# Second attention of a two-layer step in head pairs: value tiles stationary over both latent tiles, output written turned, norm weights as scales of copies

## The chip, the cores and the metric

The kernel runs on one core of one Trainium2 chip. The metric is the device time of one execution in microseconds, the median of several runs. A profiled execution gives the span, the busy time of each engine and the rows quoted below.

## The reference

Two token streams go through two layers: 128 prompt tokens and 256 sample tokens, 1024 features, all in fp32. Layer 0 mixes with a gated long convolution and grouped attention. Layer 1 mixes with latent attention (MLA), and each layer ends with 16 experts, two per token. What matters here is the mixer of layer 1:

```python
c_q, c_kv, k_rope = split(h @ od_w_in)                # 256, 128, 32
c_q, c_kv = rmsnorm(c_q, gq), rmsnorm(c_kv, gkv)
q = rmsnorm((c_q @ w_uq).reshape(n, 16, 96), q_norm)
k_nope, v = split((c_kv @ w_ukv).reshape(n, 16, 128)) # 64 and 64 per head
k = rmsnorm(concat(k_nope, broadcast(k_rope)), k_norm)
q, k = rope_tail(q, 64), rope_tail(k, 64)             # sample tokens only, last 32
o = softmax(q @ k.T * 96 ** -0.5) @ v                 # prompt: 128 keys; sample: 128 cached + 256
y = o.reshape(n, 1024) @ od_w_out
```

Prompt tokens see the 128 prompt keys. Sample tokens see 128 cached keys (made from a cached latent and a cached rotary part, without rotation) and their own 256.

## The kernel before

Five engines run instruction lists written by hand, joined by semaphores. Tokens stand in three tiles of 128: tile 0 is the prompt, tiles 1 and 2 are the sample (here "latent tiles"). PSUM has eight banks; `Banks.stage` (lines 174 to 184) lists which bank each job takes, `claim` (818) makes TensorE wait until its last user has drained it, and `filled_wait`, `drained_wait` and `drain_inc` are the other ends. Matmuls all pass through `product` (line 841), transposes ("turns") through `turn` (848) and ScalarE's plain copies through `copy_out` (1500), so these lines gather many jobs in the profile; the tile names tell them apart. An fp32 product leaves two records in the trace, a turn one.

Weights come in pieces of 1 MB through a ring of nine slots on SyncE's queue, each sent when the piece nine before it has been used (lines 654 to 658); `send_early` (660) puts five pieces of expert weights into the arena, in layer 1 once the attention's last results (`mO3`) are drained.

The stage of interest starts behind the norm of the latents (DVE lines 2402 to 2412). TensorE turns the latents (`cT`), then works on four groups of four heads (`HG`). `project(g)` (1406) makes queries (3 tiles of 384 columns, two contraction steps) and keys (4 tiles of 256 columns) of group g; ScalarE copies them into `q4s[g % 2]` and `k4s[g % 2]`. VectorE's `mla_norm` (1918) has 12 steps: square and sum of queries and of keys (steps 0 to 3, with the rotary part of the keys copied in first), reciprocal of the root (4), and then `mla_turn` (624): on the keys a product with the reciprocal, one with the weights of the norm, and the rotation of two tiles (8 to 11); GpSimd does the same on the queries (4 to 7). `MLA_NORM_AT` (85) says behind which unit of the present group's attention each step for the next group stands in VectorE's queue.

In group g TensorE makes the values (`project_kv(g, "mv", ...)`), waits for `qk_ready` and `qk_turned`, turns 12 query and 16 key tiles of 128x96, waits for ScalarE's copies of these, projects group g+1 and then runs `attention` (958) over 12 units (tile, head). A unit is: scores (queries stationary, 128 or 384 keys moving), maximum on VectorE (1873), exp with a sum on ScalarE (1551), turn of the probabilities on TensorE, copy to SBUF on VectorE (1868), and the product with the values: the turned probabilities are stationary and 64 value columns move, one product per key tile. Behind the fourth head of a tile VectorE divides by the sums (1884) and writes tokens by features into `mtok`. Each stage has two buffers. One step of the modulation products (`mod_step("mla", ...)`, 1024x512 weights) stands behind unit 3 of each group; it also has a selecting part of 16 narrow records.

After the last group 24 turns and six copies bring `mtok` into `hT`, features by tokens (1457 to 1464), and `moe(1)` begins with the output product (`out_tile`, 921), prompt tile first.

Layer 0's attention (`pair_scores`, `pair_turn`, `tile_values`, `sums_turn`, `sums_spread`, lines 996 to 1031, and `tile_mask`, `tile_join` on VectorE) already goes by pairs of heads: the values are stationary, 64 wide, in two halves of the array, and the probabilities of four heads (512 columns) move. The result comes out turned, so the division needs the sums along the columns: reciprocals are turned, masked into eight rows and spread over 128 partitions by a product with `half_rows`.

## Time and profile before

| | |
|---|---|
| median of 3 runs | 1047.16 us |
| range of the runs | 1043.32 to 1048.2 us |
| the profiled execution | 1041.73 us |
| its span | 1039.9 us |
| mean granted clock of TensorE | 0.898 of 2.4 GHz |
| busy: TensorE, VectorE, ScalarE, GpSimd | 875.4, 397.9, 270.3, 92.7 us |
| second attention, first key or query turned to first output product | 614.8 to 789.7 us |

The busy times are sums over stages with different limits, and idle time of an engine costs only where another waits for it. A timeline row gives the start and length of a run of like instructions; the bracket behind it is the idle time before it and what ended that.

### The profile page before, as it was taken

The page shows a single profiled execution, that of the slowest core. Times are in us where ns is not written, and L with a number is a line of the kernel's source. Part 1 is how long each engine was busy: PE and PEld are TensorE (multiplying, and loading weights), DVE is VectorE, ACT ScalarE, POOL GpSimd, SP SyncE. Part 2 cuts the span into 40 slices and gives each one's busy share as a digit, 9 for nine tenths or more (in the row PEclk, how much of TensorE's full clock was granted, in tenths as well). Part 3 has the DMA queues.
Part 4 walks back from the last instruction along what each step waited for, and adds up shares of the span by engine and source line. Part 5 has one row for each costly group of instructions (what it writes and reads, how often), then busy time and mean ns, then how long its engine had stood idle before and what let it go on. Part 6 is the DMA issues. An engine that isn't in the chain of part 4 may idle for free.

```text
span 1039.9 us, 12183 instructions
## 1 busy us (share of the span) xinstructions
PE 875.4 (84%) x4419; PEld 509.4 (49%) x4419; DVE 397.9 (38%) x854; ACT 270.3 (26%) x624; POOL 92.7 (9%) x120
## 2 busy tenths in 40 slices
PE   2898999998989979997767778878789999998760
PEld 0345765535534555553324446656675565554320
DVE  1468182353342424221115157383732342321114
ACT  1134012200531332221124244333341232221111
POOL 1000000000000030000030032130300012000002
PEclk9997999999889979999966898887879987999995
DMA  8980244344900499999999462020106188999975
GB/s 237 382 283 1 81 128 162 110 162 108 380 38 1 158 336 380 413 411 410 367 393 390 150 243 81 1 82 1 41 1 243 65 316 299 397 411 411 388 267 192
DMA packets 86417, 231.79 MB, mean 223 GB/s; under 512 B 8832, under 2 KB 18561, under 8 KB 86041
## 3 DMA queue, kind: packets, MB, share of 16 engines
q1 hardware_dynamic: 72418, 193.88, 50.5%
q0 software_dynamic: 7616, 26.95, 7.3%
q10 hardware_dynamic: 6328, 10.23, 2.7%
q8 instruction: 35, 0.57, 0.2%
q14 instruction: 20, 0.16, 0.0%
HBM read 216.40 MB, written 17.52 MB: 225 GB/s over the span
## 4 chain that ended last, share of the span: by engine, by line
PE 60%; DMA 16%; DVE 8%; issue 5%; ACT 5%; DVEq 3%; SPq 2%; ACTq 1%; POOLq 0%; POOL 0%
PE ps L841 54%; DMA ring<-in_moe_w_up_dram 7%; DMA ring<-in_w_mod_dram 5%; PE ps L848 4%; DVEq L1805 3%; DMA arena<-in_moe_w_up_dram 2%; SPq L658 1%; PE ps L1044 1%; ACT arena L1500 1%; ACTq L641 1%; DMA arena<-in_moe_w_down_dram 1%; ACT hT L1531 1%; DMA hT<-h_rows,rows_in 1%; DVE negmax L1873 1%; DVE statA L1938 1%
## 5 line engine op out<-in xcount | busy, mean ns | idle before, releaser
L841 PE MATMUL ps<-arena 128*64 128x256 f32 (+12 forms) x1332 | 290.6, 445 | 39.1 <-DVE arena L1868 10.6
L841 PEld LDWEIGHTS ps<-arena 128*64 128x64 f32 (+4 forms) x1332 | 170.6, 188 | 141.9 <-issue 68.5
L841 PE MATMUL ps<-ring,hT 128*128 128x512 f32 (+2 forms) x384 | 136.8, 517 | 7.8 <-ACT hT L1531 3.6
L841 PE MATMUL ps<-ring,arena 128*64 128x256 f32 (+1 forms) x864 | 125.0, 432 | 16.3 <-DMA ring<-in_moe_w_up_dram 8.3
L841 PEld LDWEIGHTS ps<-ring,hT 128*128 128x128 f32 x384 | 74.7, 196 | 66.4 <-issue 61.5
L841 PEld LDWEIGHTS ps<-ring,arena 128*64 128x64 f32 x864 | 60.8, 136 | 66.1 <-issue 39.6
L841 PE MATMUL ps<-ring,condT 128*32 128x512 f32 x384 | 63.9, 784 | 25.2 <-DMA ring<-in_w_mod_dram 19.1
L1500 ACT ACTIVATE arena<-ps 128x256 f32<-128x256 f32 (+6 forms) x94 | 43.9, 497 | 133.4 <-PE ps L841 120.5
L848 PE MATMUL ps<-ident,arena 128*128 128x128 f32 (+2 forms) x276 | 51.7, 319 | 24.9 <-ACT arena L1551 11.0
L2139 DVE TENSOR_TENSOR arena<-arena,ps 128x128 f32<-128x128 f32 x37 | 10.6, 288 | 138.1 <-ACT arena L1578 138.1
L841 PE MATMUL ps<-hT,ring 128*128 128x384 f32 x192 | 62.1, 486 | 0.0
L848 PEld LDWEIGHTS ps<-ident,arena 128*128 128x128 f32 (+2 forms) x276 | 37.2, 163 | 36.3 <-issue 22.9
L2142 DVE COPY arena<-ps 64x512 f32<-64x512 f32 x37 | 25.7, 693 | 65.7 <-PE ps L841 65.7
L841 PEld LDWEIGHTS ps<-hT,ring 128*128 128x128 f32 x192 | 36.5, 190 | 25.2
L1584 ACT ACTIVATE arena<-ps 64x512 f32<-64x512 f32 x37 | 21.8, 589 | 78.2 <-PE ps L841 78.2
L1873 DVE TENSOR_REDUCE negmax<-ps 128x1 f32<-128x384 f32 (+1 forms) x48 | 22.0, 462 | 51.2 <-PE ps L841 50.4
L841 PEld LDWEIGHTS ps<-ring,condT 128*32 128x32 f32 x384 | 11.0, 128 | 61.3 <-issue 30.7
L1551 ACT ACTIVATE arena<-ps,negmax 128x384 f32<-128x384 f32 (+1 forms) x48 | 24.3, 508 | 63.6 <-DVE negmax L1873 63.4
L1578 ACT ACTIVATE arena<-ps 128x128 f32<-128x128 f32 x37 | 10.3, 277 | 90.7 <-PE ps L841 90.7
L1958 DVE TENSOR_TENSOR arena<-ps,gb 128x512 f32<-128x512 f32 x12 | 8.3, 691 | 63.4 <-PE ps L841 63.4
L1531 ACT ACTIVATE hT<-ps,modT,modA 128x128 f32<-128x128 f32 x48 | 17.7, 464 | 45.4 <-PE ps L848 42.5
L641 POOL DMA_DIRECT2D arena<-in_before_dram x2 | 1.1, 563 | 313.0 <-DVE hT L1967 313.0
(284 smaller groups left out, 918.5 us busy)
## 6 DMA issues: line engine op xcount, KB each, us to landing
ring<-in_w_mod_dram SPq DMA_DIRECT2D x48, 1024.0 KB, 10.4
ring<-in_moe_w_down_dram SPq DMA_DIRECT2D x24, 1024.0 KB, 18.1
ring<-in_moe_w_gate_dram SPq DMA_DIRECT2D x42, 512.0 KB, 14.0
ring<-in_moe_w_up_dram SPq DMA_DIRECT2D x42, 512.0 KB, 16.5
arena<-in_moe_w_gate_dram SPq DMA_DIRECT2D x32, 512.0 KB, 8.0
arena<-in_moe_w_up_dram SPq DMA_DIRECT2D x32, 512.0 KB, 9.9
arena<-in_moe_w_down_dram SPq DMA_DIRECT2D x13, 1024.0 KB, 13.4
ring<-in_ev_w_in_dram SPq DMA_DIRECT2D x9, 1024.0 KB, 12.3
```

The lines of the kernel that those rows point to most:

```text
L641: eng.dma_start(dst, src).then_inc(s, 16)
L658: sp.dma_start(ring_view(i, shape, off)[rows], src).then_inc(piece_full[i % RING], 16)
L841: mm = pe.matmul(out, lhsT, rhs, **kw)
L848: mm = pe.transpose(out, src, ident[:, :])
L1500: drain_inc(act.activation(dst, src, kw.pop("func", ACT.Copy), **kw), stage, i)
L1531: ins = act.activation(hT[:, k, t * P:(t + 1) * P], bank[:, k * P:(k + 1) * P], ACT.Identity, bias=modT[:, l, SH2 if which else SH1, k, GR ...
L1551: ins = act.activation(pr[:, i % 2, 0:nk], bank[:, 0:nk], ACT.Exp, bias=negmax[:, i:i + 1], accum_out=psumexp[:, i:i + 1])
L1584: act.activation(dst, ps[Y_BANKS[e % 2]][0:HALF, :], ACT.Copy).then_inc(done[l], 1)
L1805: dve.drain()
L1873: dve.tensor_reduce(negmax[:, i:i + 1], bank[:, 0:nk], AXX, ALU.max, negate=True).then_inc(negmax_ready, 1)
L2139: dve.tensor_tensor(mid[:, e % 2, :], sil[:, e % 2, :], ps[GU_BANKS[e % 2]][:, P:2 * P], ALU.mult).then_inc(mid_ready[l], 1)
L2142: dve.tensor_copy(dst, ps[Y_BANKS[e % 2]][HALF:P, :]).then_inc(y_read[1][l], 1)
```

## The change

It touches layer 1's mixer only.

- Attention goes by six pairs of heads per group, `MLA_PAIRS` = (tile, pair): both prompt pairs first, then tiles 1 and 2 of pair 0, then of pair 1. Each engine has its own `mla_attention` with the order of rounds written out. Scores have four banks in place of two.
- The turned probabilities are kept for both latent tiles (`turned_m`), and one product per key tile and head has the values as the stationary operand, 64 wide in one half of the array, and 256 columns moving (`mla_values`). The prompt's are 128 wide (`mla_values_prompt`).
- The result comes out as features by tokens and is written straight into `hT` (`mla_join`); `mtok`, its 24 turns and six copies are gone, and `out_tile` waits for `mO` itself. The division by the sums goes as in layer 0: reciprocal, turn, mask, spread, copy, join, once for the prompt and once for the latent tiles of a group.
- Of the copies of turned probabilities, the second of every odd pair is ScalarE's.
- The norm weights of the first 64 features, and 96 ** -0.5, are no longer multiplied in by VectorE and GpSimd: they are a scale by partition (`head_gain`) of the copies of turned queries and keys. The rotary weights are folded into tables made once (`mla_tables`): `kp`, the keys' rotary part with weight and rotation, `kp2`, its sum of squares, and `qtab`, the queries' rotation table. `mla_norm` has 7 steps, which cover 64 of the 96 features of a key. The loads of norm weights grow by two: `mgain` is loaded as two rows of 32, `head_gain` as two columns.
- Keys are turned before queries, `project(g+1)` comes before the wait for the copies, the last two key copies are VectorE's, there is one buffer each for queries and keys, and the modulation step stands at the end of a group's attention, between the turn of the sums and the last value products.

The core of the diff (views of buffers, banks, loads and removed bodies are left out):

```diff
-MLA_NORM_STEPS = 12
-MLA_NORM_AT = {1: (0,), 2: (1,), 3: (2,), 4: (3,), 7: (4,), 8: (8,), 9: (9,), 10: (10,), 11: (11,)}
+MLA_NORM_STEPS = 7
+MLA_NORM_AT = {0: 0, 1: 1, 2: 2, 3: 3, 5: 4, 6: 5, 7: 6}
 MLA_AHEAD = 3
+MLA_PAIRS = [(0, 0), (0, 1), (1, 0), (2, 0), (1, 1), (2, 1)]
+MLA_KEYS = (3, 1, 2)
...
+def mla_column(i, r):
+    t, p = MLA_PAIRS[i]
+    return 4 * r + 2 * p + (QH + t - 1 if t else 0)
+def mla_turned(g, i, r, src):
+    t, p = MLA_PAIRS[i]
+    if t == 0:
+        return hT[:, 2 * g + p, P + P * r:2 * P + P * r], src
+    return turned_m[:, p, :, r, P * (t - 1):P * t], src.rearrange("p (a b) -> p a b", b=P)
...
-            for step in range(4, 8):
-                mla_turn(pool, g, step, (msq[:, 0, :, 0:ROPE], msq[:, 1, :, 0:ROPE]))
-                if step == 7:
-                    pool.drain().then_inc(qk_turned, 1)
-                else:
-                    pool.drain()
+            flat = q4.rearrange("p t h e -> p (t h) e")
+            pool.tensor_tensor(flat, flat, statA[:, 1, 0:NT * HG].unsqueeze(2).broadcast_to([P, NT * HG, QK]), ALU.mult)
+            for t in range(1, NT):
+                pool.drain()
+                rope(pool, q4[:, t, :, NOPE:QK], qtab[:, t - 1, :, :], mrb[:, 0, :, :], mrb[:, 1, :, :], HG, ROPE)
+            pool.drain().then_inc(qk_turned, 1)
...
+        else:
+            for g in range(NHG):
+                drained_wait(pe, f"mO{g}", min(t, 1))
...
+    def mla_scores(g, i):
+        t, p = MLA_PAIRS[i]
+        for r in range(2):
+            bank = claim(f"mS{g}", 2 * i + r)
+            keys = k4T[:, 2 * p + r, 0, :] if t == 0 else k4T[:, 2 * p + r, 1:4, :].rearrange("p a b -> p (a b)")
+            fill_inc(product(bank[:, 0:P if t == 0 else T], q4T[:, t, 2 * p + r, :], keys, start=True, stop=True), f"mS{g}", 2 * i + r)
+    def mla_turns(g, i):
+        for r in range(2):
+            bank = claim(f"mPT{g}", 2 * i + r)
+            drained_wait(pe, f"mS{g}", 2 * i + r)
+            for s in range(1 if MLA_PAIRS[i][0] == 0 else NT):
+                mm = turn(bank[:, s * P:(s + 1) * P], mprobs[:, i % 2, r, s * P:(s + 1) * P])
+            fill_inc(mm, f"mPT{g}", 2 * i + r)
+    def mla_values_prompt(g):
+        for u in range(4):
+            drained_wait(pe, f"mPT{g}", u)
+        bank = claim(f"mO{g}", 0)
+        for p in range(2):
+            for r in range(2):
+                mm = product(bank[HD * r:HD * r + HD, P * p:P * p + P], v4[:, 0, 2 * p + r, :], hT[:, 2 * g + p, P + P * r:2 * P + P * r], start=True, stop=True)
+        fill_inc(mm, f"mO{g}", 0)
+    def mla_values(g, p):
+        for u in range(4 * p + 4, 4 * p + 8):
+            drained_wait(pe, f"mPT{g}", u)
+        bank = claim(f"mO{g}", 1) if p == 0 else ps[B[f"mO{g}", 1][0]]
+        for s, t in enumerate(MLA_KEYS):
+            for r in range(2):
+                mm = product(bank[HD * r:HD * r + HD, NSA * p:NSA * p + NSA], v4[:, t, 2 * p + r, :], turned_m[:, p, s, r, :], start=s == 0, stop=s == NT - 1)
+        if p == 1:
+            fill_inc(mm, f"mO{g}", 1)
+    def mla_sums_turn(g, part):
+        pe.wait_ge(sums_ready, NT + 2 * g + part + 1)
+        fill_inc(turn(claim(f"mL{g}", 2 * part)[0:QH, 0:P], rinv[:, 0:QH]), f"mL{g}", 2 * part)
+    def mla_sums_spread(g, part):
+        n = 512 if part else NSA
+        fill_inc(product(claim(f"mL{g}", 2 * part + 1)[:, 0:n], half_rows, masked_m[:, 0:n], start=True, stop=True), f"mL{g}", 2 * part + 1)
+    def mla_attention(g):
+        n = len(MLA_PAIRS)
+        for i in range(n + 2):
+            if i >= 2:
+                mla_turns(g, i - 2)
+            if i == 5:
+                mla_sums_spread(g, 0)
+                mla_scores(g, i)
+            if i == 4:
+                mla_sums_turn(g, 0)
+                mla_values_prompt(g)
+            if i == 6:
+                mla_values(g, 0)
+        mla_sums_turn(g, 1)
+        mod_step("mla", MLA_AHEAD + g)
+        mla_values(g, 1)
+        mla_sums_spread(g, 1)
...
-        q4, k4 = q4s[g % 2], k4s[g % 2]
         project_kv(g, "mv", NOPE)
         pe.wait_ge(qk_ready, NT + 1 + g)
+        for s, t in enumerate((0,) + MLA_KEYS):
+            bank = claim(f"mkT{g}", s)
+            for h in range(HG):
+                mm = turn(bank[0:QK, h * P:(h + 1) * P], k4[:, t, h, :])
+            fill_inc(mm, f"mkT{g}", s)
         pe.wait_ge(qk_turned, g + 1)
         for t in range(NT):
             bank = claim(f"mqT{g}", t)
             for h in range(HG):
                 mm = turn(bank[0:QK, h * P:(h + 1) * P], q4[:, t, h, :])
             fill_inc(mm, f"mqT{g}", t)
-        for s, t in enumerate((0, 3, 1, 2)):
-            bank = claim(f"mkT{g}", s)
-                mm = turn(bank[0:QK, h * P:(h + 1) * P], k4[:, t, h, :])
-            fill_inc(mm, f"mkT{g}", s)
+        if g + 1 < NHG:
+            project(g + 1)
         for t in range(NT):
             drained_wait(pe, f"mqT{g}", t)
         for t in range(NT + 1):
             drained_wait(pe, f"mkT{g}", t)
-        if g + 1 < NHG:
-            project(g + 1)
         for t in range(NT + 1):
             drained_wait(pe, f"mv{g}", t)
-        attention(str(g), units_mla, HG, lambda t, h: q4T[:, t, h, :],
-                  lambda t, h: k4T[:, h, 0, :] if t == 0 else k4T[:, h, 1:4, :].rearrange("p a b -> p (a b)"),
-                  lambda t, h: [v4[:, s, h, :] for s in ((0,) if t == 0 else (3, 1, 2))])
-    for g in range(NHG):
-        for t in range(NT):
-            drained_wait(pe, f"mO{g}", t)
-    for t in range(NT):
-        for q in range(2):
-            bank = claim("moT", 2 * t + q)
-                mm = turn(bank[:, c * P:(c + 1) * P], mtok[:, t, (4 * q + c) * P:(4 * q + c + 1) * P])
-            fill_inc(mm, "moT", 2 * t + q)
-    for i in range(2 * NT):
-        drained_wait(pe, "moT", i)
+        mla_attention(g)
...
+    def mla_probs(g, i):
+        nk = P if MLA_PAIRS[i][0] == 0 else T
+        for r in range(2):
+            u, c = 2 * i + r, mla_column(i, r)
+            act.wait_ge(negmax_ready, 2 * NPAIRS + 2 * len(MLA_PAIRS) * g + u + 1)
+                filled_wait(act, f"mPT{g}", u - 4)
+            drain_inc(act.activation(mprobs[:, i % 2, r, 0:nk], bank_of(f"mS{g}", u)[:, 0:nk], ACT.Exp, bias=negmax[:, c:c + 1], accum_out=psumexp[:, c:c + 1]), f"mS{g}", u)
+    def mla_copy(g, i):
+        nk = P if MLA_PAIRS[i][0] == 0 else T
+        copy_out(f"mPT{g}", 2 * i + 1, *mla_turned(g, i, 1, bank_of(f"mPT{g}", 2 * i + 1)[:, 0:nk]))
+    def mla_reci(g, part):
+        n = 512 if part else NSA
+        if g or part:
+            drained_wait(act, f"mO{g if part else g - 1}", 1 - part)
+        copy_out(f"mL{g}", 2 * part + 1, reci_m[:, 0:n], bank_of(f"mL{g}", 2 * part + 1)[:, 0:n])
+    def mla_attention(g):
+        n = len(MLA_PAIRS)
+        for i in range(n + 2):
+            if i >= 2 and i % 2:
+                mla_copy(g, i - 2)
+            if i == 5:
+                mla_reci(g, 0)
+            if i < n:
+                mla_probs(g, i)
+            if g + 1 < NHG and i == 4:
+                mla_root(g + 1)
+        mod_step("mla", MLA_AHEAD + g)
+        mla_reci(g, 1)
...
+        for s in range(2):
+            copy_out(f"mkT{g}", s, k4T[:, :, s, :], bank_of(f"mkT{g}", s)[0:QK, :].rearrange("p (a b) -> p a b", b=P), scale=head_gain[:, 2:3])
         for t in range(NT):
-            copy_out(f"mqT{g}", t, q4T[:, t, :, :].rearrange("p a b -> p (a b)"), bank_of(f"mqT{g}", t)[0:QK, :])
-        for s in range(NT + 1):
...
+    def mla_max(g, i):
+        nk = P if MLA_PAIRS[i][0] == 0 else T
+        for r in range(2):
+            c = mla_column(i, r)
+            bank = filled_wait(dve, f"mS{g}", 2 * i + r)
+            dve.tensor_reduce(negmax[:, c:c + 1], bank[:, 0:nk], AXX, ALU.max, negate=True).then_inc(negmax_ready, 1)
+    def mla_copy(g, i):
+        nk = P if MLA_PAIRS[i][0] == 0 else T
+        for r in range(2 - i % 2):
+            bank = filled_wait(dve, f"mPT{g}", 2 * i + r)
+            drain_inc(dve.tensor_copy(*mla_turned(g, i, r, bank[:, 0:nk])), f"mPT{g}", 2 * i + r)
+    def mla_sums(g, part):
+        last = 2 * len(MLA_PAIRS) if part else 4
+        for u in (last - 2, last - 1):
+            drained_wait(dve, f"mS{g}", u)
+        dve.reciprocal(rinv[:, 0:QH], psumexp[:, QH * part:QH * part + QH]).then_inc(sums_ready, 1)
+    def mla_mask(g, part):
+        bank = filled_wait(dve, f"mL{g}", 2 * part)
+        columns = own_column if part else own_column[:, 0::2]
+        n = 4 if part else 2
+        shape = [QH, n, P]
+        drain_inc(dve.tensor_tensor(masked_m[:, 0:n * P].rearrange("p (a b) -> p a b", b=P), bank[0:QH, 0:P].unsqueeze(1).broadcast_to(shape),
+                                    columns.unsqueeze(2).broadcast_to(shape), ALU.mult), f"mL{g}", 2 * part)
+    def mla_join(g, part):
+        bank = filled_wait(dve, f"mO{g}", part)
+        drained_wait(dve, f"mL{g}", 2 * part + 1)
+        n = NSA if part else P
+        by_head = lambda a: a[:, 0:2 * n].rearrange("p (a b) -> p a b", b=n)
+        cols = slice(P, T) if part else slice(0, P)
+        drain_inc(dve.tensor_tensor(hT[:, 2 * g:2 * g + 2, cols], by_head(bank), by_head(reci_m), ALU.mult), f"mO{g}", part)
+    def mla_attention(g):
+        n = len(MLA_PAIRS)
+        for i in range(n + 2):
+            if i == 6:
+                mla_join(g, 0)
+            if i >= 2:
+                mla_copy(g, i - 2)
+            if i == 3:
+                mla_sums(g, 0)
+                mla_max(g, i)
+            if i == 4:
+                mla_mask(g, 0)
+            if i == 7:
+                mla_sums(g, 1)
+            if g + 1 < NHG and i in MLA_NORM_AT:
+                mla_norm(g + 1, MLA_NORM_AT[i])
+        mla_mask(g, 1)
+        mod_step("mla", MLA_AHEAD + g)
+        mla_join(g, 1)
...
-        q4, k4 = q4s[g % 2], k4s[g % 2]
         flat = lambda a: a.rearrange("p t h e -> p (t h) e")
+        k_nope = flat(k4)[:, :, 0:NOPE]
+        by_nope = msq[:, 0:nkk * NOPE].rearrange("p (a e) -> p a e", e=NOPE)
+        by_key = lambda which: statA[:, which, nq:nq + nkk].rearrange("p (t h) -> p t h", h=HG)
         settle()
         if step == 0:
             for t in range(NT):
                 drained_wait(dve, f"mq{g}", t)
-            for t in range(NT + 1):
-                kr = kr_c if t == NT else um[:, t, QR + KVR:ODD_IN]
-                dve.tensor_copy(k4[:, t, :, NOPE:QK], kr.unsqueeze(1).broadcast_to([P, HG, ROPE]))
-            dve.tensor_tensor(flat(msq)[:, 0:nq, :], flat(q4), flat(q4), ALU.mult)
+            dve.tensor_tensor(msq.rearrange("p (a e) -> p a e", e=QK), flat(q4), flat(q4), ALU.mult)
         elif step == 1:
-            dve.tensor_reduce(statA[:, 0, 0:nq], flat(msq)[:, 0:nq, :], AXX, ALU.add)
+            dve.tensor_reduce(statA[:, 0, 0:nq], msq.rearrange("p (a e) -> p a e", e=QK), AXX, ALU.add)
         elif step == 2:
             for t in range(NT + 1):
                 drained_wait(dve, f"mk{g}", t)
-            dve.tensor_tensor(flat(msq), flat(k4), flat(k4), ALU.mult)
+            dve.tensor_tensor(by_nope, k_nope, k_nope, ALU.mult)
         elif step == 3:
-            dve.tensor_reduce(statA[:, 0, nq:nq + nkk], flat(msq), AXX, ALU.add)
+            dve.tensor_reduce(statA[:, 0, nq:nq + nkk], by_nope, AXX, ALU.add)
+            settle()
+            dve.tensor_tensor(by_key(0), by_key(0), kp2.unsqueeze(2).broadcast_to([P, NT + 1, HG]), ALU.add)
             settle()
             dve.tensor_scalar(statA[:, 0, 0:28], statA[:, 0, 0:28], 1.0 / QK, EPS, ALU.mult, ALU.add).then_inc(qvar, 1)
         elif step == 4:
             dve.wait_ge(qroot, 2 + g)
             dve.reciprocal(statA[:, 1, 0:28], statA[:, 1, 0:28]).then_inc(inv_root, 1)
+        elif step == 5:
+            dve.tensor_tensor(k_nope, k_nope, statA[:, 1, nq:nq + nkk].unsqueeze(2).broadcast_to([P, nkk, NOPE]), ALU.mult)
+        else:
+            shape = [P, NT + 1, HG, ROPE]
+            dve.tensor_tensor(k4[:, :, :, NOPE:QK], kp.unsqueeze(2).broadcast_to(shape), by_key(1).unsqueeze(3).broadcast_to(shape), ALU.mult)
+            dve.drain().then_inc(qk_ready, 1)
...
+    mla_tables()
     for step in range(MLA_NORM_STEPS):
         mla_norm(0, step)
+    for i in range(MLA_AHEAD):
+        mod_step("mla", i)
     for g in range(NHG):
-        attention(str(g), units_mla, HG,
-                  lambda t, g=g: mtok[:, t, g * HG * VD:(g + 1) * HG * VD].rearrange("p (h e) -> p h e", e=VD))
+        for s in range(2, NT + 1):
+            bank = filled_wait(dve, f"mkT{g}", s)
+            drain_inc(dve.tensor_scalar(k4T[:, :, s, :], bank[0:QK, :].rearrange("p (a b) -> p a b", b=P), head_gain[:, 2:3], None, ALU.mult), f"mkT{g}", s)
+        mla_attention(g)
```

## Rows read from the trace of the kernel before

**Rows 1.** The page's 40 slices of 26 us: busy share of the DMA engines, in tenths.
```profile
DMA  8980244344900499999999462020106188999975
```

**Rows 2.** Stretches of the second attention, busy us of each engine, clock, DMA share, GB/s.
```profile
core 0: us, PE busy (x) PEld busy (x) DVE busy (x) ACT busy (x) POOL busy (x), PEclk, DMA share, GB/s
583.60:614.80 31.20, 23.31 (x108) 12.18 (x108) 20.14 (x26) 10.30 (x23) 10.22 (x12) 0.89 0.74 267
614.80:663.40 48.60, 40.71 (x199) 30.41 (x200) 26.46 (x51) 19.68 (x46) 10.39 (x10) 0.79 0.13 47
663.40:711.40 48.00, 39.72 (x200) 29.02 (x199) 26.70 (x51) 18.38 (x46) 10.39 (x10) 0.82 0.13 44
711.40:759.20 47.80, 39.09 (x199) 28.36 (x198) 26.46 (x51) 18.36 (x46) 10.39 (x10) 0.82 0.07 23
759.20:789.70 30.50, 26.17 (x177) 22.32 (x176) 12.79 (x33) 14.03 (x38) 0.00 (x0) 0.89 0.09 26
```

**Rows 3.** TensorE's waits in the second group, 663.4 to 711.4: total us, times, longest.
```profile
PE ps L841 <- DVE arena L1868: 3.8, 3, 1.7
PE ps L848 <- ACT arena L1551: 3.1, 5, 1.1
PE ps L841 <- ACT arena L1500: 1.2, 1, 1.2
```

**Rows 4.** The chain that ended last: a steady head of the last group; layer 1's output products.
```profile
777.26 0.34 PE ps L848 x3
777.60 1.26 PE ps L841 x8
...
789.72 27.70 PE ps L841 x64
```

**Rows 5.** Timeline of layer 0's value products, TensorE: start, us, instruction.
```profile
295.07 1.08 PE L841 MATMUL ps<-arena,cv 128*64 128x512 f32 x4
295.98 1.89 PE L841 MATMUL ps<-arena 128*64 128x512 f32 x8
```

**Rows 6.** Timeline, TensorE: a modulation step's two parts.
```profile
604.62 1.92 PE L841 MATMUL ps<-ring,condT 128*32 128x512 f32 x16
...
633.48 2.08 PE L841 MATMUL ps<-rowsel,modrow 128*64 128x2 f32 x16
```

**Rows 7.** Groups of the second group's stretch, shapes apart: busy us, mean ns, idle before.
```profile
L1868 DVE COPY arena<-ps 128x384 f32<-128x384 f32 x8 | 4.4, 550 | 0.4 <-PE ps L841 0.2 <-issue 0.2
...
L633 POOL TENSOR_TENSOR arena<-arena 128x1152 f32<-128x1152 f32 x1 | 4.0, 3953 | 0.1
...
L633 DVE TENSOR_TENSOR arena<-arena 128x1536 f32<-128x1536 f32 x1 | 3.1, 3076 | 0.1
...
L631 DVE TENSOR_TENSOR arena<-arena,statA 128x1536 f32<-128x1536 f32 x1 | 2.5, 2531 | 0.1
...
L631 POOL TENSOR_TENSOR arena<-arena,statA 128x1152 f32<-128x1152 f32 x1 | 2.1, 2112 | 36.9 <-DVE statA L1943 36.9
...
L1936 DVE TENSOR_TENSOR arena<-arena 128x1536 f32<-128x1536 f32 x1 | 1.8, 1757 | 0.3 <-issue 0.3
...
L1539 ACT ACT_TABLE_LOAD x1 | 1.3, 1283 | 0.0
```

**Rows 8.** Timeline of the lead-in: a load on GpSimd, VectorE's first norm step, TensorE's first turns.
```profile
538.07 0.58 POOL L641 DMA_DIRECT2D arena<-in_rope_m_dram  x1
...
595.18 0.81 DVE L1929 COPY arena<-arena 128x128 f32<-128x128 f32 x4 [9.51 <-ACT arena L1500]
...
609.27 1.99 PE L841 MATMUL ps<-arena 128*128 128x256 f32 x8 [0.69 <-ACT gb L1500]
614.82 4.93 PE L848 MATMUL ps<-ident,arena 128*96 128x128 f32 x28 [3.55 <-DVEq L1948]
```

**Rows 9.** Timeline of the stage's end: last division, turns, first output product.
```profile
784.98 0.42 DVE L1884 TENSOR_TENSOR xn<-ps,rinv 128x256 f32<-128x256 f32 x1 [0.89 <-PE ps L841]
...
785.66 2.81 PE L848 MATMUL ps<-ident,xn 128*128 128x128 f32 x24 [0.71 <-DVE xn L1884]
...
789.72 1.53 PE L841 MATMUL ps<-ring,hT 128*128 128x512 f32 x3 [1.25 <-ACT hT L1500]
```

**Rows 10.** The stretch of layer 0's attention, columns as in rows 2.
```profile
270.00:311.00 41.00, 34.32 (x143) 15.26 (x142) 21.51 (x53) 16.14 (x56) 0.00 (x0) 0.79 0.46 181
```

197 lines of the change are left out of this document (56 added, 141 removed).

## The prediction

> **What bounds the kernel now.** I began with the page's table of 40 slices [rows 1]: the DMA engines stand at 9 from about 365 us and at 8 or 9 again from about 830 us, in the two expert stages; between 575 and 780 us the digits are 0 to 6, mostly 0 to 2. The second attention is not a transfer stage. The stretches [rows 2] cut it at the first turned query of each group of four heads: 31.2 us of lead-in, three groups of 48.6, 48.0 and 47.8, and 30.5 to the first output product, 206.1 us together. In a group TensorE is busy 40 of 48 us, VectorE 26.5, ScalarE 18 to 20, GpSimd 10.4. So TensorE bounds the group, but not at its full pace: the granted clock is 0.79 to 0.82, and since it has two levels, 2.4 and 1.2 GHz, a mean of 0.82 is 36% of the time at the lower. That is 17 us of each 48, and 62 us from 614.8 on (20.4+17.3+17.2+6.7). The waits of one group [rows 3] name VectorE's copies of the turned probabilities (3.8 us), the exps (3.1) and the copies of the keys (1.2). VectorE is late because the next group's norm work (squares, sums, scale, gain, rotation) stands in its queue between a maximum and a copy. In the last group, which has no norm work, a head of a latent tile takes a steady 1.60 us [rows 4].
>
> **TensorE's work, at full clock.** 64 records of 512 columns take 27.70 us [rows 4], 0.433 each; a product of fp32 is two records, so 384 columns cost 0.64, 256 cost 0.43, 128 cost 0.21. In 1.60 us a head does three turns (0.35), a score product (0.64) and three value products [rows 4], which leaves 0.61 for those: 0.20 each for 64 moving columns.
> Removed: per group 8x0.61 + 4x0.20 = 5.7 us of value products. Added: the values are stationary, 64 wide, with 256 moving columns. Layer 0 has this form: 8 records of 64x512 took 1.89 us and 4 took 1.08 [rows 5], about 0.22 a record, half of 0.433, so the two halves of the array work at once. 256 columns are then 0.11 a record, 24 records of the latent tiles 2.6 us, the prompt's 0.5. Nearly half is saved there, but the sums of the exps must now be turned and spread (two turns at 0.25, a spread of 512 columns at 0.87 and one of 256 at 0.43: 1.8 us together). Scores (8x0.64+4x0.21=6.0), turns of probabilities (3.3), of queries and keys (3.3), the value projection (1.7), the next projections (5.5) and the modulation (1.92 and 2.08 [rows 6] and 0.2) stay. Per group: 6.0+3.3+3.3+1.7+5.5+4.2+3.1+1.8 = 28.9 us, against 29.7 before. The work hardly shrinks; the gain must come from waits and clock.
>
> A rule of the Trainium skill speaks against the change (TensorEngine Tiling (Array Packing), Key Properties): a change of tiling mode drains TensorE. Layer 0's rows after such a change [rows 5] show 1.08 us for four records where 0.87 is the steady price, so 0.2 at most. With six changes a group the rule at that price would put 4.8 us on the sum.
>
> **VectorE and GpSimd.** VectorE loses the gain of the keys (3.08 us), a third of their squares and sums (1.2 of twice 1.76), three of twelve copies of probabilities (1.4 at 0.55 and less) [rows 7], both rotations and the copies of the rotary part (about 3); it gains two copies of turned keys (0.7 each, the 0.55 of 384 columns scaled to 512), the mask and wider joins (0.8 more). From 26.5 [rows 2] it comes to about 20. GpSimd loses the gain (3.95). ScalarE takes the three copies and two of reciprocals: plus 2.5 on 18 to 20, hidden beside TensorE. The scale factor within copies costs nothing: the copy is there already, and it streams the same elements; were a scaled copy dearer by a tenth, 0.3 us a group, it would lie beside the projections. The tables built once (some 24 small VectorE operations, 3.5 us at 0.15 each) fall into a wait of VectorE of 9.51 us [rows 8]. The two further small loads of weights are issued on GpSimd's queue near 538 us, at 0.58 each [rows 8], and wanted at 583: 44 us of cover; beyond it, each microsecond late is one lost.
>
> **The first start.** Before, TensorE was free at 609.27+1.99 = 611.26 and waited until 614.82 for the rotations [rows 8]. Root and reciprocal come about 1.5 us earlier, at 602; of GpSimd's 10.4 us a group [rows 2] 3.95 go, so it is done by 610 with its pauses, and the keys, turned first now, by 606. The start moves to 611.3: 3.5 saved.
>
> **One group in queue order.** I set out the new instructions of each engine in their order, with the durations above, 0.2 us for a hand-over to TensorE, 0.12 to VectorE, 0.15 to ScalarE (before: maximum to exp 0.04 to 0.2, exp to turn 0.1 to 0.3). TensorE then waits: 0.9 for the first exps; 1.5 for the second pair's, whose maxima stand behind the square of the queries (1.35 us, three quarters of the 1.76 [rows 7]); 1.1 and 0.9 for the third's and fourth's, behind a sum and the squares of the keys; 1.1 for the mask, before the prompt's spread; 1.9 for a copy that ScalarE does after its change of tables for the root (2x1.28 us [rows 7]); 2.6 for the last reciprocal, behind the scale of the keys on VectorE. Together 10.0, and 28.9+10.0 = 38.9 us a group. Before, by the same procedure, 43.6. The wait for the key copies ahead of the projections (1.2 [rows 3]) is gone, since the projections now come first. The tail of the last group (sums, mask, spread, copy, join) is followed by the prompt's output product, which doesn't need it.
> The old stage's end: last join, 24 turns and six copies, 784.98 to 789.72 [rows 9], 4.7 us, falls away whole. The last group has no norm, root or projection: 3.2 for turns, 1.0 for their copies, 16.4 for attention and half a modulation, 1.8 of waits: 22.4.
> At full clock: 27.7 + 3x38.9 + 22.4 = 166.8 us. The old one by this procedure was 31.2 (measured) + 160.1; measured were 174.9 for the latter, so 14.8 us are the price of 62 us at the low clock, 0.24 per us. In the new stage the ladder's beginning and the narrow modulation products will still bring the clock down; the stretch of some 10 us at a low clock after each group's late copies and 64-column values should go in part. I take 40 us, 9.6 us of price. The stage: 166.8+9.6 = 176.4, against 206.1: 29.7 saved.
> The bounds: waits of 6 to 14 us a group (12 each way), 15 to 75 us at the low clock (3.6 to 18 us). Extremes are 47 and 9 saved; 8 in 10 I set at 15 to 43.
>
> **What follows the stage.** The expert stage starts its transfers when output weights are freed and when the last join is done, so it moves as a block. The early weights (asked for right after the last join before, ahead of the output products) start some 5 us later against them; they are wanted over 60 us later.
>
> **The total.** The profiled execution took 1041.73 us, its span 1039.9, 5.4 below the median of 1047.16. It would come to 1012; from the median, 1047.2-29.7 gives 1017.5, which I forecast, with 1004 to 1032. A measurement of this kernel tells about 0.5%, 5 us, from no change.
>
> **Rivals.** (a) The pair form carries its own stalls. Layer 0's attention took 41.0 us for 24 head tiles at a clock of 0.79 [rows 10], 20.5 for twelve. Without its packed rows the scores cost 3 more, the modulation 4.2, norm and root about 4, the rest of the group 10.5: 42.2, and with the mask and norms colliding 45. Then 3.5 + 3x3.1 + 5.5 = 18 saved: 1029. For it: the same order of work on VectorE. Against: the join and ScalarE's copy of the reciprocals come earlier in the round here. Chance 0.25. (b) The clock stays up and the waits stay at 6: 42 saved, 1005; chance 0.12. (c) The expert stage, at a DMA share of 9 in [rows 1], gives most of it back, as its transfers can't come earlier: 1040; against it, every such transfer waits for an event of this stage. Chance 0.04. (d) Slower: the clock. With TensorE's gaps short but frequent, it could stay at 1.2 GHz through all four rounds. From 166.8, the gain of 39 is used up when 164 us at the low clock cost 0.24 each; where TensorE has no wait left to cover it the price is 0.5, and 80 us suffice. All four attention parts at the low clock double some 18 us of work each, 74 us, less some 24 of waits that this swallows: 50, and 1047-39+50 = 1058. The rows speak against so much: projections ran at full clock in every group. Chance 0.02. (e) That it doesn't do what it says: the turned result would need another pass; the join writes straight into the tile that the output product reads, so this gets no chance. The forecast has the remaining 0.57; the range leaves out c, d and about half of b.
> The Trainium skill (SBUF — State Buffer, Who interferes with whom) has VectorE and GpSimd lock each other out of a shared port. The keys' scale of 2.53 us beside GpSimd's 2.11 agrees, against 1.76 for a product as large alone [rows 7]; by full exclusion the new scale would wait 2.1 us, 1.3 more than I took, 5 us in all.
>
> **What would show it.** Right: turns of keys at 611 us with no wait for GpSimd; groups of 40 to 44 us; value products of 64x256 at 0.11 a record at full clock; the first output product 2 us or less after the last spread; VectorE near 20 us a group; the expert stage unchanged in length. Wrong: groups over 45; waits over 3 us for the mask, the join or ScalarE's table change; a mean clock at 0.75 or less; a longer expert stage.
> Chances: faster by over 0.5%, 0.94 (forecast, a, b, and most of c); within 0.5%, 0.04; slower 0.02.

## The result, and the profile after

In four runs each the changed kernel took **1000.19 us** (995.23 to 1004.56), the kernel before 1045.24 (1040.76 to 1048.2): ratio 0.957, 95% interval 0.951 to 0.963. The forecast was 1017.5, its range 1004 to 1032: the change gave more than the range held. Ratios leave out two slow runs of the experiments: one of the kernel before (1055.34 us, beside x1 to x4) and one of x14 (1002.6 us). The profiled execution of the changed kernel took 1004.56 us, its span 1002.7. The page's granted clock and DMA lines, 40 slices of 25 us:

```profile
PEclk9997999999888997999885679998998998999995
DMA  7990236235850088999989946112106289999975
```

The groups lie in the 25th to 30th slice, where DMA stands at 0 to 2 but for the first; the clock is at 9 there, once at 8, and its low digits 5, 6, 7 stand ahead of them. The stretches, columns as in [rows 2]: to the first turned latent, the lead-in, the four groups, the rest.

```profile
0.00:592.05 592.05, 508.80 (x2385) 277.68 (x2386) 219.55 (x479) 138.81 (x316) 32.60 (x54) 0.91 0.66 237
592.05:617.13 25.08, 24.20 (x108) 13.16 (x109) 12.43 (x32) 9.88 (x22) 5.18 (x9) 0.81 0.69 245
617.13:654.96 37.83, 32.56 (x181) 21.20 (x180) 20.47 (x39) 20.66 (x51) 6.10 (x9) 0.95 0.33 117
654.96:693.70 38.74, 34.04 (x182) 21.84 (x181) 20.48 (x39) 19.49 (x50) 6.11 (x9) 0.91 0.16 55
693.70:730.32 36.62, 32.44 (x182) 21.22 (x181) 20.52 (x39) 19.38 (x50) 6.11 (x9) 0.95 0.09 31
730.32:755.49 25.17, 22.78 (x135) 15.11 (x133) 12.56 (x31) 11.83 (x35) 0.00 (x0) 0.92 0.01 1
755.49:1002.70 247.21, 196.68 (x1157) 106.06 (x1156) 68.13 (x171) 51.23 (x110) 20.96 (x28) 0.91 0.83 314
```

From here "the stage" runs from the first turned latent to the first output product: 163.4 us here, 203.9 before (585.78 to 789.72). The 40.5 us divide into the lead-in 4.0 (29.0 before by this cut), three groups 31.2 (144.4 to 113.2) and the last group 5.3 (30.5 to 25.2).

What changed inside the three groups? With the low clock counted as in the prediction, they had 54.9 us of it before (20.4+17.3+17.2) and have 14.5 now. Busy time less half the low time is TensorE's work at full rate: 92.0 us before, 91.9 now. So the work is the same within what this reckoning can tell (three profiles of the changed kernel give 91.9, 91.1 and 92.6); 20.2 us of the difference are booked under the clock and 10.7 under pauses (24.9 to 14.2). This is bookkeeping: a pause that the low clock hides comes back at full clock, so taking the low clock away gives less than half of its time, as the prices below show. What the form of the value products saves in work (2.8 us a group by x3 below) is spent again, on turning and spreading the sums among others; the gain is made elsewhere.

The second group of the changed kernel, TensorE's timeline (start, length, instruction, idle time before it):

```profile
664.97 0.65 PE L845 MATMUL ps<-ident,arena 128*128 128x128 f32 x2 [0.29 <-ACT arena L1557]
665.46 1.46 PE L838 MATMUL ps<-arena 96*128 96x384 f32 x4
668.21 0.53 PE L845 MATMUL ps<-ident,arena 128*128 128x128 f32 x2 [1.29 <-DVE hT L1882]
...
671.02 0.87 PE L845 MATMUL ps<-ident,arena 128*128 128x128 f32 x6 [0.99 <-DVE hT L1882]
...
677.44 2.93 PE L838 MATMUL ps<-arena 96*128 96x384 f32 x4
680.16 1.49 PE L845 MATMUL ps<-ident,arena 128*128 128x128 f32 x6
681.80 2.24 PE L838 MATMUL ps<-xn,arena 128*64 128x256 f32 x12 [0.16 <-DVE hT L1904]
```

Four score records take 1.46 us at full clock and 2.93 at the low one; here the low stretch is some 7 us, behind pauses of 1.29, 0.99, 0.77 and 0.70 us. The same four pauses stand in the second group of x13, another profile of the same kernel, and there the clock stays at 1.00: the pauses alone don't settle it.

### The profile page after: what moved, and what is told of

Same layout as the page of the kernel before. It is cut to its first block, busy times and chain, and to the rows that moved or that the text cites. A ratio compares the mean times of both kernels' runs of the same rounds, so it can differ in the third digit from the quotient of the medians.

```text
span 1002.7 us, 11944 instructions
## 1 busy us (share of the span) xinstructions
PE 851.5 (85%) x4323; PEld 476.3 (47%) x4323; DVE 374.1 (37%) x829; ACT 271.3 (27%) x630; POOL 77.1 (8%) x118
## 4 chain that ended last, share of the span: by engine, by line
PE 63%; DMA 18%; DVE 7%; issue 4%; ACT 3%; SPq 2%; ACTq 2%; DVEq 1%; POOLq 0%; POOL 0%
PE ps L838 56%; DMA ring<-in_w_mod_dram 5%; DMA ring<-in_moe_w_up_dram 5%; PE ps L845 4%; DMA ring<-in_moe_w_down_dram 2%; DMA h_rows<-xn 2%; DMA arena<-in_moe_w_up_dram 2%; PE ps L1067 2%; ACTq L636 1%; SPq L653 1%; DVE negmax L1876 1%; DVEq L1826 1%; ACT hT L1540 1%; DMA hT<-h_rows,rows_in 1%; DVE xn L1882 1%
## 5 line engine op out<-in xcount | busy, mean ns | idle before, releaser
L838 PE MATMUL ps<-arena 128*64 128x256 f32 (+13 forms) x1108 | 244.6, 462 | 20.5 <-DVE arena L2082 5.2
L838 PEld LDWEIGHTS ps<-arena 128*64 128x64 f32 (+4 forms) x1108 | 127.5, 172 | 114.9 <-issue 71.7
L838 PE MATMUL ps<-ring,arena 128*64 128x256 f32 (+1 forms) x864 | 129.7, 444 | 16.4 <-DMA ring<-in_moe_w_down_dram 8.4
L838 PE MATMUL ps<-ring,condT 128*32 128x512 f32 x384 | 59.9, 737 | 26.9 <-DMA ring<-in_w_mod_dram 20.5
L1509 ACT ACTIVATE arena<-ps 128x256 f32<-128x256 f32 (+5 forms) x88 | 39.2, 452 | 132.6 <-PE ps L838 123.8
L845 PEld LDWEIGHTS ps<-ident,arena 128*128 128x128 f32 (+2 forms) x332 | 41.4, 148 | 38.8 <-issue 18.5
L2207 DVE TENSOR_TENSOR arena<-arena,ps 128x128 f32<-128x128 f32 x37 | 10.7, 288 | 131.6 <-ACT arena L1602 131.6
L838 PEld LDWEIGHTS ps<-hT,ring 128*128 128x128 f32 x192 | 36.6, 190 | 25.1
L838 PEld LDWEIGHTS ps<-ring,condT 128*32 128x32 f32 x384 | 10.4, 121 | 61.7 <-issue 28.4
L838 PE MATMUL ps<-xn,arena 128*64 128x256 f32 (+2 forms) x144 | 35.7, 496 | 1.8 <-DVE hT L1904 1.6
L1540 ACT ACTIVATE hT<-ps,modT,modA 128x128 f32<-128x128 f32 x48 | 17.7, 463 | 45.3 <-PE ps L845 42.4
## 6 DMA issues: line engine op xcount, KB each, us to landing
ring<-in_moe_w_up_dram SPq DMA_DIRECT2D x42, 512.0 KB, 16.3
ring<-in_ev_w_in_dram SPq DMA_DIRECT2D x9, 1024.0 KB, 13.5
```

What stands on the lines that cost most here:

```text
L838: mm = pe.matmul(out, lhsT, rhs, **kw)
L845: mm = pe.transpose(out, src, ident[:, :])
L1509: drain_inc(act.activation(dst, src, kw.pop("func", ACT.Copy), **kw), stage, i)
L1540: ins = act.activation(hT[:, k, t * P:(t + 1) * P], bank[:, k * P:(k + 1) * P], ACT.Identity, bias=modT[:, l, SH2 if which else SH1, k, GR ...
L2207: dve.tensor_tensor(mid[:, e % 2, :], sil[:, e % 2, :], ps[GU_BANKS[e % 2]][:, P:2 * P], ALU.mult).then_inc(mid_ready[l], 1)
```

## The experiments

Two theories of why the clock was low before: **A**, TensorE stalls behind VectorE's norm work; **B**, the value products with 64 moving columns. Each ratio is against the runs of the kernel before in the same job on the same chip. The table sums up; "low" is time at the low clock and "pauses" TensorE's idle time, both in the four groups. Stage, low and pauses come from one profile each, and the changed kernel's own three differ by 14 us in low and by 3.6 in the stage: smaller differences than these show nothing by themselves.

| kernel | median us | ratio | stage | low | pauses |
|---|---|---|---|---|---|
| before | 1045.24 | 1 | 203.9 | 61.6 | 29.3 |
| changed | 1000.19 | 0.957 | 163.4 | 18.5 | 16.6 |
| x1 the same | 996.32 | 0.954 | 163.7 | 20.9 | 16.2 |
| x13 the same | 1000.31 | 0.957 | 160.1 | 6.9 | 18.2 |
| x2 VectorE later | 1009.6 | 0.967 | 171.6 | 27.1 | 24.0 |
| x3 64 columns | 1015.78 | 0.974 | 189.7 | 54.5 | 14.2 |
| x6 128 columns | 983.21 | 0.942 | 170.2 | 12.9 | 14.2 |
| x7 x2 and x3 | 1020.48 | 0.977 | 196.3 | 65.0 | 18.1 |
| x4 turns at the end | 1006.88 | 0.964 | 171.6 | 24.5 | 19.7 |
| x5 before, 128 columns | 1038.46 | 0.994 | 199.3 | 45.9 | 28.0 |
| x9 before, no gain | 1019.02 | 0.973 | 190.2 | 43.9 | 25.4 |
| x10 before, projections first | 1040.52 | 0.995 | 202.6 | 64.2 | 25.3 |
| x11 x5, x9 and x10 | 1006.75 | 0.962 | 176.0 | 16.3 | 21.4 |
| x8 modulation before sums | 1001.17 | 0.959 | 164.8 | 23.9 | 15.2 |
| x12 norm later | 998.56 | 0.953 | 156.0 | 10.1 | 13.6 |
| x14 the same | 995.41 | 0.951 | 156.4 | 11.2 | 13.5 |
| x15 x12 and x8 | 1002.78 | 0.959 | 164.8 | 29.5 | 12.6 |

In x3, x6, x7, x9 and x11 the hidden state is another than the reference's, and the experts' plan makes fewer blocks from it: behind the stage 1108 TensorE instructions and 237.3 us in x3, 1059 and 225.5 in x6, against 1157 and 247. There only the stage is compared.

**x1, the changed kernel again.**

> The changed kernel once more, as the measure for the others. Its profile gave 163.4 us from the first turned latent to the first output product (203.9 before), with 18.5 us at the low clock in the four groups (61.6 before). If the shorter stage is not chance, the stage comes out at 160 to 167 us again and the clock of the four groups at 0.91 or more; if the clock was luck, a group should show 0.85 or less.

996.32 us, stage 163.7, 20.9 us low: the result stands.

**x2, VectorE late again**: four more products of 1024 elements in each of three groups.

```diff
@@ mla_norm, step 5 and step 6
+    if g:
+        for _ in range(2):
+            settle()
+            dve.tensor_tensor(by_nope, by_nope, by_nope, ALU.max)
```

> Four more VectorE products of 1024 elements (1.23 us each alone) beside the norm steps 5 and 6 of each next group, so that VectorE is about as late as before the change; nothing else differs. Theory A (the low clock before came from the stalls that VectorE's norm work made): the groups get longer by more than the waits, since the clock falls as well: 5 us a group, 12 to 20 us in all, and at least 15 us more at the low clock. Theory B (the low clock came from the form of the value products): only waits, 2 to 3 us a group, 6 to 9 us in all, and the clock stays at 0.91 or more.

The stage grew by 7.9 us, to 171.6, the pauses by 7.8 and the low clock by 6.2. But the edit touches the three groups only, and these grew by 11.1 us (113.7 to 124.8): pauses 7.8 more, low clock 9.7 more, their clock 0.89; the lead-in and the last group, which it leaves alone, were 3.2 shorter. The medians, 1009.6 and 996.32 in one job, lie 13.3 apart. That is between the two theories: more than B allows, less low clock than A asks for, and the 9.7 us are within what profiles of one kernel differ by. TensorE's largest wait in the three groups of x2 (total us, times, longest):

```profile
PE ps L845 <- DVE rinv L1888: 11.6, 3, 3.9
```

The same wait in the changed kernel:

```profile
PE ps L845 <- DVE rinv L1888: 2.8, 3, 1.2
```

VectorE in the second group of x2, with the added products of step 5 (L1989) and step 6 (L1996) about the last reciprocal:

```profile
681.30 2.62 DVE L1989 TENSOR_TENSOR arena<-arena 128x1024 f32<-128x1024 f32 x2
...
684.30 0.19 DVE L1888 RECIPROCAL rinv<-psumexp 128x8 f32<-128x8 f32 x1
...
685.36 2.62 DVE L1996 TENSOR_TENSOR arena<-arena 128x1024 f32<-128x1024 f32 x2
```

Only the two products of step 5, 2.6 us, stand in front of the last reciprocal, and the wait for it grew by 2.9 us a group: they are waited for in full. The two of step 6 stand behind it, beside TensorE's modulation step, and the waits for the mask behind them stayed at 1.4 us. So late norm work costs pauses where a reciprocal stands behind it; what it does to the clock this run leaves open, and x9 takes it up.

**x3, the old form of the value products** in the otherwise changed kernel.

```diff
@@ mla_values (the prompt's likewise)
-                mm = product(bank[HD * r:HD * r + HD, NSA * p:NSA * p + NSA], v4[:, t, 2 * p + r, :], turned_m[:, p, s, r, :], ...)
+                mm = product(bank[:, c:c + HD], turned_m[:, p, s, r, P * n:P * n + P], v4[:, t, 2 * p + r, :], ...)
```

> Value products in the old form, turned probabilities stationary and 64 value columns moving, in the new order of rounds and with the new waits. The result then stands as tokens by features where the join takes features by tokens, so this part of the output is not the reference's. Theory B: 2.5 us more work a group and the clock falls by as much as before: 8 us a group, 25 to 35 us in all. Theory A: the work alone, 2.5 us a group at most, 6 to 11 us in all, clock nearly as it is.

The stage grew by 26.0 us: pauses 2.0 fewer, low clock 33.6 us more (16.8 by halves), work at full rate some 11 more (2.8 a group, near the prediction's 5.7 against 3.1). Theory B had 25 to 35, theory A 6 to 11: it is B. The timeline of x3, first group:

```profile
633.47 2.93 PE L838 MATMUL ps<-arena 96*128 96x384 f32 x4
...
637.84 5.35 PE L838 MATMUL ps<-arena,xn 128*128 128x64 f32 x24 [0.16 <-DVE hT L1906]
...
644.90 3.00 PE L838 MATMUL ps<-ring,condT 128*32 128x512 f32 x16
```

The clock was low already for the four score records (2.93 us) ahead of the values; it stayed low through these and into the modulation. In the changed kernel's first group it was low there too, and the 12 value records behind took 1.51 us, at full clock.

**x6, the same with 128 columns a record**, so that against x3 nothing but the width of the latent value products differs.

```diff
-    mm = product(bank[:, c:c + HD], ..., v4[:, t, 2 * p + r, :], ...)
+    mm = product(bank[:, c:c + 2 * HD]..., ..., v4[:, t, h:h + 2, :], ...)
```

> The kernel of x3 (the changed kernel with the latent value products in the old form), with 128 moving columns a record instead of 64; part of the values is overwritten, so the attention's result is not the reference's. x3 had a stage of 189.7 us (from the first turned latent to the first output product) with 54.5 us at the low clock in its groups, x1 163.7 with 20.9. Theory B: the low clock falls to 20 to 30 us, the stage to 173 to 178. Theory C (number of records): it stays at 50 or more, and the stage at 188 to 193. The expert stage depends on the values (the number of blocks that its plan makes), so the stage decides and not the whole time.

Twice the columns, and the stage is 19.5 us shorter, low clock 54.5 to 12.9 us. The timeline of x6, the same place and one in its second group:

```profile
632.92 2.92 PE L838 MATMUL ps<-arena,xn 128*128 128x128 f32 x24 [0.67 <-DVE hT L1907]
...
637.13 1.92 PE L838 MATMUL ps<-ring,condT 128*32 128x512 f32 x16
...
680.17 4.57 PE L838 MATMUL ps<-arena,xn 128*128 128x128 f32 x24
```

A record of 64 columns took 0.22 us at the low clock, one of 128 columns 0.12 at the full one. It isn't the number of records (24 in both) that matters. Runs of 128 columns are no guarantee either: the last row is one that ran mostly at the low clock.

**x5, the width alone in the kernel before**; `v` now holds heads h and h+1, so each head also writes the next one's place, which the next head then overwrites.

```diff
-    mm = product(bank[:, h * HD:(h + 1) * HD], pT[:, j % 2, kt, :], v, ...)
+    mm = product(bank[:, h * HD:(h + 2) * HD]..., pT[:, j % 2, kt, :], v, ...)
```

> The kernel before; each value product moves 128 columns instead of 64 (its own head's values and, beside them, the next head's, or its own again for the fourth head), so it makes the same result and writes as much again that the next head's product overwrites. The number of records and the loads of weights stay. Theory B (the low clock comes from the 64 moving columns of the value products, their form): at full clock a value product costs the same, 0.20 us, since 128 columns cost 0.21; the 61.6 us at the low clock in the four groups should fall to 20 to 35, at about half a microsecond each the stage loses 12 to 18 of its 203.9 us, and the run comes to 1027 to 1033. Theory A (stalls behind VectorE's norm work bring the clock down) and a third, C (the number of records, each with its load of weights, does it): low clock stays at 55 to 65 us and the run at 1042 to 1050.

Ratio 0.994 (0.992 to 0.997), the stage 4.6 us shorter, its four groups 5.9. Wider products do make it faster, but by a third of what B said: 45.9 us at the low clock remain. Each of the 15.7 that went brought 5.9/15.7 = 0.38 us; the wider products' own cost is in this (a steady head takes 1.64 us for 1.60), so that the clock's share is a little more. That the kernel is faster its seven runs show; the 15.7 us alone would hardly stand out from the 14 between profiles of one kernel.

**x9, no norm-weight products in the kernel before**, on VectorE and on GpSimd (`mla_turn`, part 1, cut to two elements).

> The kernel before without the products with the norm weights of the queries and keys (VectorE's 3.08 and GpSimd's 3.95 us a group become two elements each), so the weights of these norms are left out of what it computes. If VectorE's lateness costs waits, as in x2 (7.9 us for three times 5.1 us of extra work), each group gains about 1.5 us and the lead-in about 3, since the rotations come earlier: the stage goes from 203.9 to about 196, the run to 1036. Rival: in the groups VectorE's norm work is hidden, and only the lead-in gains: stage 201, run 1041. In both the low clock of the groups stays at 55 to 65 us, since the form of the value products stays. The expert stage may have another number of blocks, so the stage decides.

The stage fell by 13.7, 2.1 of it in the lead-in and 11.7 in the groups; pauses 3.9 fewer, low clock 17.7 us fewer. Both expectations were off, in the stage and in the low clock: the norm work has its part in the low clock of the old form, so A holds beside B. One profile shows it, and x11 bears it out.

**x10, projections ahead of the waits for the key copies** in the kernel before.

> The kernel before, with the next group's projections ahead of the waits for the copies of the turned queries and keys. Expected: the wait for the key copies (1.2 us in a group) is hidden by the projections' 6.7 us, 3.6 less in all: stage 200, run 1040. Rival: the attention then waits as long for the last copy or the value copies, or the projections' banks collide: no change, 1044.

Ratio 0.995 (0.991 to 0.998), stage 1.3 shorter. The three groups lose 4.1 us (3.6 expected), and the waits for ScalarE's copies in all four go from 4.9 us to 1.5; the lead-in and the last group, at clocks of 0.84 and 0.86 where before had 0.89, take 2.7 more. The low clock as a whole stays, at 64.2 us.

**x11, the three together.**

> x5, x9 and x10 in one: the old form of one head of one tile at a time, with 128 moving columns a value product, without the products with the norm weights, and with the projections first. If the three only add: 4.6 (measured in x5) plus about 7.5 plus 3.6, stage 188, run 1028. If the low clock is brought on by narrow products and by gaps together, it falls below x5's 45.9 us, to 25 to 35, and the stage to 180 to 185. What is then left against the changed kernel's 163.7 is what only the pairs give (the turns at the end, 8.2, the packed halves and the shorter chain of one unit).

In the three groups the parts alone take off 6.7, 11.7 and 4.1 us, 22.5 in sum; together it is 26.5. The low clock falls to 16.3 us, by 45.3, where the parts alone took off 15.7 and 17.7 and x10 nothing: that is lower than the 25 to 35 expected if both causes work together. The stage is 27.9 shorter. The three groups of x11:

```profile
617.52:656.65 39.13, 33.50 (x199) 25.23 (x199) 23.50 (x51) 19.67 (x48) 6.60 (x10) 0.96 0.27 95
656.65:695.78 39.13, 33.75 (x199) 25.30 (x198) 23.77 (x51) 18.40 (x47) 6.62 (x10) 0.96 0.16 55
695.78:735.42 39.64, 33.61 (x199) 25.35 (x198) 23.52 (x51) 18.38 (x47) 6.61 (x10) 0.96 0.08 27
```

48 us became 39 with the old one-head units. The changed kernel's stage is another 12.5 shorter: 6.1 in the last group, where the turns were, 4.7 in the three groups, 1.8 in the lead-in.

**x7, x2 and x3 together**, the way back.

> x2 and x3 together: the changed kernel with the latent value products in the old form (64 moving columns) and with two more VectorE products of 1024 elements at each of two norm steps; the attention's result is not laid out as the reference's. If the two costs add, the stage is x3's 189.7 plus x2's 7.9, 197.6 us, with 55 to 65 us at the low clock; that would be within some 6 us of before's 203.9, the missing part being the turns at the end (8.2 in x4) less what the first start gave. If the late VectorE acts through the clock, which is low in x3 already, it adds less, 190 to 193.

196.3, against a sum of 197.6. Its groups last 45.3, 48.7 and 49.7 us, 143.7 together, where the kernel before has 144.4. The sums agree, the parts don't: work 97.5 us for 92.0, pauses 15.7 for 24.9, low clock 61.2 for 54.9. Narrow values and a late VectorE bring the old length and the old low clock back, by another way; that the lengths meet within 1 us is chance.

```profile
608.82:654.12 45.30, 38.47 (x205) 26.73 (x204) 25.52 (x43) 20.87 (x51) 10.15 (x9) 0.89 0.28 98
654.12:702.86 48.74, 43.66 (x205) 30.21 (x204) 25.69 (x43) 19.43 (x49) 10.16 (x9) 0.74 0.13 44
702.86:752.56 49.70, 45.91 (x205) 33.20 (x204) 25.51 (x43) 19.54 (x49) 10.18 (x9) 0.74 0.07 22
```

**x4, the 24 turns and six copies put back** behind the last join.

> Behind the last group TensorE waits for both joins, turns 24 tiles of 128x128 into banks and waits for six ScalarE copies of 512 columns, as the kernel before did; the copies go to free space, so the output is the reference's. Both theories: the chain of spread, copy and join (about 1.5 to 2 us) and the old 4.7 us come back, 6 to 7 us in all, at an unchanged clock. If the output product hides part of it, less than 4.

The last group takes 33.25 us against 25.2: 8.1 more (6 to 7 expected), with a clock of 0.85 in it. The timeline:

```profile
750.11 2.07 PE L839 MATMUL ps<-arena,filtc 8*128 8x512 f32 x2
753.81 4.83 PE L846 MATMUL ps<-ident,xn 128*128 128x128 f32 x24 [1.64 <-DVE hT L1917]
759.95 3.24 PE L839 MATMUL ps<-ring,hT 128*128 128x512 f32 x7 [1.30 <-issue]
```

The turns ran at the low clock, 4.83 us where they took 2.81 before [rows 9]: that is the size that was missed.

**x8, the modulation step ahead of the second sums**: a candidate.

```diff
-                mla_sums_turn(g, 1)
                 mod_step("mla", MLA_AHEAD + g)
+                mla_sums_turn(g, 1)
```

> A candidate to beat both: the changed kernel, in which TensorE does the modulation step ahead of turning the second sums, so that it works while VectorE makes their reciprocal, instead of waiting. The four waits for the reciprocal were 3.2 us together in x1; the mask has then only the second pair's value products (1.5 us) beside it. Expected: those waits at 0, none at the spread, 3.2 us less than the changed kernel, about 993 us beside its 996.3 of x1 (ratio 0.951). Rival: the wait moves to the mask or to ScalarE's copy of the modulation, 996 or more.

The four waits for the reciprocal are gone (3.2 to 0); those for the mask rose by 0.7, for VectorE's copies by 1.3, the low clock by 3 us, each against x1. Stage 164.8: nothing gained.

**x12, x14: the norm steps a round later**; step 6 now stands behind `mla_mask(g, 1)`, and the second pair of lines is ScalarE's root. x13 is the changed kernel in x14's job.

```diff
-MLA_NORM_AT = {0: 0, 1: 1, 2: 2, 3: 3, 5: 4, 6: 5, 7: 6}
+MLA_NORM_AT = {1: 0, 2: 1, 3: 2, 4: 3, 6: 4, 7: 5}
-                    if g + 1 < NHG and i == 4:
+                    if g + 1 < NHG and i == 5:
```

> A candidate to beat both: the changed kernel with VectorE's norm steps put one round later (squares of the queries in round 1, their sums in 2, the keys' in 3 and 4, the reciprocal in 6, the scale of the keys in 7 behind the reciprocal of the sums, the rotary part behind the mask), and ScalarE's root one round later. The waits of x1 for the turned copies in the second and third round (5.1 us) and for the last reciprocal (3.2, of which 0.4 in the last group) come from the squares, sums and the scale ahead of them. Expected: 4 to 5 us less, stage 159, run 992. Rival: squares and sums now delay the copies of the latent pairs, which are three times as long, or the queries' rotation on GpSimd is late for their turns: stage 163 or more, run 996 to 1001.

> The changed kernel as it is, on the same chip as x14 and x15. Expected: 996 to 1000 us, stage 163 to 164 with 18 to 21 us at the low clock in its groups; if the low clock differs from execution to execution, the stage lies between 158 and 168.

> x12 once more beside the changed kernel. If the 7.7 us of its profile are in every execution: 7 to 8 us below x13, stage 156. Rival: the clock in the groups is a matter of the single execution, and without it only the waits' 2.6 us are gained: 2 to 3 us below x13, stage between 156 and 162.

The stage is 156.0 and 156.4 us, shorter than in all three profiles of the changed kernel (163.4, 163.7, 160.1). Against the first profile of the changed kernel the waits for the turned copies fell from 5.8 to 1.6 us in three groups, for the reciprocal from 2.8 to 1.4; those for the exps rose from 2.0 to 4.3, since ScalarE's second load of tables now stands ahead of the next group's first exp. In the medians it is 4.9 us below x13 in one job, but the ratios, 0.951 (0.948 to 0.955) and 0.957 (0.954 to 0.961), just overlap, and with all six of its runs x14 has 0.953: the stage is shown shorter, by two profiles against three; the whole is likely so, by less than the 7 to 8 us expected. The first two groups of x12:

```profile
613.17:648.07 34.90, 30.78 (x181) 20.20 (x180) 21.20 (x39) 19.41 (x50) 6.09 (x9) 1.00 0.35 127
648.07:682.98 34.91, 30.80 (x181) 20.25 (x180) 21.21 (x39) 19.47 (x50) 6.10 (x9) 1.00 0.17 61
```

These are at full clock, as are two groups of x13 (below, 36.9 and 36.6 us): the work is the same, 30.8 and 31.0, and the pauses are 4.1 for 5.9 and 5.6. So the shift saves some 1.6 us a group by pauses alone, about 5 in three groups, where the stages differ by 3.7 to 7.7.

**x15, x12 with x8.**

> x14 with TensorE's modulation step ahead of the turn of the second sums. x12's waits for the reciprocal were 1.8 us in four; they should go, and 1.5 us with them: stage 154.5, 1 to 2 us below x14. Rival, as in x8: the pauses only move to the mask (2.1 in x12), and the clock falls more often: no gain against x14.

The fewest pauses of all (12.6 us) and more low clock than x12 (29.5), stage 164.8: the rival came true. Fewer pauses alone don't keep the clock up.

## Why the prediction was wrong

**The steps that failed** are two terms of the stage: the waits of a group, set at 10.0 us and measured at 5.9 and 5.6 at full clock, and the time at the low clock, taken as 40 us and measured at 18.5. The median missed the forecast by 17.3 us: 10.9 of these are in the stage, 1.9 in the kernel before (1045.24 in this comparison, 1047.16 when the forecast was made) and 4.5 outside the stage, where no cause is shown. Of the 10.9 the groups at full clock gave 6.3 (waits 4.2 a group less, TensorE's work 2.1 more than reckoned) and the low clock 4.9; without the 6.4 us beside the stage the time would have been 1006.6, inside the range.

x13 allows the reckoning at full clock, as the prediction made it. Its last three stretches:

```profile
652.90:689.83 36.93, 30.99 (x181) 20.25 (x180) 20.49 (x39) 19.41 (x50) 6.11 (x9) 1.00 0.16 57
689.83:726.40 36.57, 30.99 (x181) 20.22 (x180) 20.48 (x39) 19.41 (x50) 6.11 (x9) 1.00 0.09 31
726.40:749.71 23.31, 20.91 (x135) 14.58 (x133) 12.56 (x31) 11.86 (x35) 0.00 (x0) 1.00 0.01 1
```

In the prediction's own cut the stage of the first profile was 165.5 us (590.0 to 755.5) for a forecast of 176.4. The 10.9 us divide as follows; the three groups at full clock and the last group are x13's, so the low clock's part is the remainder between two profiles:

| term | forecast | measured |
|---|---|---|
| lead-in to the first turned key | 27.7 | 27.1 |
| three groups at full clock | 3x38.9 | 3x36.8 |
| last group | 22.4 | 23.3 |
| low clock | 40 us x 0.24 = 9.6 | 18.5 us, 4.7 (what is left) |
| stage | 176.4 | 165.5 |

**The waits were too long.** "TensorE then waits: ... Together 10.0": at full clock they are 5.9 and 5.6 a group in x13, and TensorE's work is 31.0 instead of 28.9. The surplus is spread over small terms, among them: the projections with the prompt's scores behind them take 6.66 us for 6.4, the value projection 1.99 for 1.7, the 24 latent value records 3.0 for 2.6, the two spreads 1.81 for 1.3. x13's waits in three groups:

```profile
PE ps L845 <- DVE hT L1882: 5.6, 5, 1.3
PE ps L845 <- DVE rinv L1888: 2.8, 3, 1.2
PE ps L838 <- DVE arena L1895: 2.1, 3, 0.7
PE ps L845 <- ACT arena L1557: 2.0, 3, 1.4
PE ps L845 <- DVE xn L1882: 1.6, 3, 0.8
PE ps L838 <- DVE hT L1904: 1.5, 3, 0.7
```

Per group: first exps 0.7 (0.9 forecast), the second pair 0.9 (1.5), third and fourth 1.5 (2.0), the mask 0.7 (1.1), the join 0.5 (none), the last reciprocal 0.9 (2.6), and for ScalarE's change of tables none (1.9). The two largest terms are the most wrong: they hold 3.6 of the 4.7 us a group. ScalarE in the second group of the changed kernel:

```profile
676.82 1.28 ACT L1548 ACT_TABLE_LOAD   x1
678.11 0.23 ACT L1548 ACTIVATE statA<-statA 128x28 f32<-128x28 f32 x1
678.24 0.47 ACT L1509 ACTIVATE xn<-ps 128x384 f32<-128x384 f32 x1
678.61 0.38 ACT L1509 ACTIVATE arena<-ps 128x256 f32<-128x256 f32 x1
679.01 1.28 ACT L1557 ACT_TABLE_LOAD   x1
```

The prediction put both loads (2x1.28) ahead of the copy. Only the first stands there: the copies run with the root's tables, and the second load comes ahead of the next exp, whose scores are not there sooner.

**The clock stayed up longer.** "I take 40 us" was a choice between 15 and 75 with no row behind it; 18.5, 20.9 and 6.9 us were measured. The price was about right: 4.7/18.5 = 0.25 against 0.24, and x13's second group, 36.9 us with no low clock and 5.9 of pauses, against 38.7 with 7.0 and 4.7 gives 1.8/7.0 = 0.26. It is no constant: between x3 and x6, with 14 us of pauses in both, it was 19.5/41.6 = 0.47. What the choice missed is that two causes work together. The change removes the 64-column value products and a quarter of VectorE's work; in the kernel before each of these alone leaves 44 to 46 us at the low clock (x9, x5), and the two, with the projections first, which alone change nothing there (x10), leave 16.3 (x11). Why the low time of one kernel then varies from 6.9 to 20.9 us stays open.

**What was right.** The mechanism as a whole: TensorE's work hardly shrinks (92.0 to 91.9) and "the gain must come from waits and clock". The first turned key stands directly behind the value projection, with no wait for GpSimd. VectorE 20.5 us a group (about 20), GpSimd 6.1 (10.4 less 3.95 is 6.4), ScalarE 19.4 to 20.7, hidden; it rose by 1.0 where 2.5 was forecast. 12 value records of 64x256 took 1.52 us, 0.13 each (0.11). ScalarE's scaled copy of 512 columns took 0.68 us, a plain one before 0.61, so it is dearer by the tenth that the prediction allowed for, and held TensorE up only in the last group, 1.2 us. The spread's end and the first output product touch (753.49+2.07, 755.49). The sign "groups of 40 to 44 us" failed on the good side, with 36.6 to 38.7. The expert stage took 247.2 us against 250.2 before; with 246.8 in x10 and 252.3 in x13 the two kernels don't differ there, so the 45 us between the medians, 40.5 of them in the stage, leave 4.6 that no place is shown for. Nor is it ahead of the stage: that part took 583.8 to 593.4 us over the profiles, in kernels of both kinds.

**The rivals.** (b), "the clock stays up and the waits stay at 6", with 42 saved and a chance of 0.12, is what happened: 40.6 in the same cut, pauses of 4.7 a group, 5.6 and 5.9 at full clock. (a)'s model was layer 0's attention at a clock of 0.79 [rows 10]; here the groups run at 0.91 to 0.95. (c) and (d) left no sign. Of the two rules: 12 value records took 1.52 us where 0.11 each makes 1.3, which leaves at most 0.2 us for a change of tiling mode, as the prediction had it. The Trainium skill (TensorEngine Tiling (Array Packing), Key Properties) states the drain at such a change, and no price. x3 has no such changes in its value products, but it changes their form too: its work was 2.8 us a group more where the records' prices alone make 2.6, so no cost of the changes is seen, and none is excluded. The exclusive lock between VectorE and GpSimd (Trainium skill, SBUF — State Buffer, Who interferes with whom) is borne out, as the last section shows. In the groups it cost VectorE 0.75 us, about the 0.8 that the prediction took.

## What to carry to other kernels

Where a stage's granted clock is low, divide its length into work at full rate, half the low time and pauses before and after: here the work was equal and both other terms moved. A product with few moving columns can cost more than it takes, by the clock that it and the records behind it get (x3 and x6: 3.00 against 1.92 us for the modulation behind it); making it wider, even with columns that are thrown away, is a cheap test. Before a single profile's clock is explained, take a second one of the same kernel. And in an engine's queue, check for each instruction whether it needs the table, the copy or the scale ahead of it, before that is put on the path.

## What had not been expected of the hardware

- Twice the moving columns made a kernel faster (x5: 1038.46 us against 1043.67; x6's stage 19.5 us shorter than x3's).
- The same kernel had 20.9, 18.5 and 6.9 us at the low clock in its groups, and the stage took 163.7, 163.4 and 160.1: low time and pauses trade against each other.
- Fewer pauses can come with more low clock: x15, 12.6 and 29.5 us, against x13, 18.2 and 6.9.
- GpSimd's scale of the queries delays VectorE's scale of the keys by about their overlap. VectorE's timeline in the changed kernel, lead-in and second group:

```profile
609.84 3.18 DVE L1985 TENSOR_TENSOR arena<-arena,statA 128x1024 f32<-128x1024 f32 x1
...
682.67 1.98 DVE L1985 TENSOR_TENSOR arena<-arena,statA 128x1024 f32<-128x1024 f32 x1
```

GpSimd's at the same places:

```profile
609.84 2.11 POOL L805 TENSOR_TENSOR arena<-arena,statA 128x1152 f32<-128x1152 f32 x1 [17.83 <-DVE statA L1983]
...
681.46 2.11 POOL L805 TENSOR_TENSOR arena<-arena,statA 128x1152 f32<-128x1152 f32 x1 [32.06 <-DVE statA L1983]
```

The square of as many elements takes 1.23 us. Begun together with GpSimd's 2.11 us, the scale took 1.95 more than that; begun 1.21 behind it, with 0.90 of overlap, 0.75 more. In x12, overlaps of 1.58 and 0.54 us went with 1.43 and 0.39 more. GpSimd's own length, 2.11, didn't change; it began first or together each time.
